# Moving one gate projection among the recurrence levels from behind level 6 to behind level 8 on TensorE

## The reference, cut to what matters

```
for n, o_branch in enumerate((o_mla, o_fnet, o_diff, o_hgrn)):
    gate = sigmoid(gate_logits[..., n * D_MODEL:(n + 1) * D_MODEL])
    merged = merged + gate * (o_branch @ w_branch[l, n])
x = x + merged @ w_out[l]
```

```
cum = cumsum(log_f)
decay = exp(where(lower_tri, cum[t] - cum[s], -inf))
scores = einsum('bhtk,bhtsk,bhsk->bhts', q, decay, k)
intra = einsum('bhts,bhsv->bhtv', scores, v)
```

## Time and profile before

| | |
|---|---|
| median of three runs | 1210.43 us (lowest 1210.18, highest 3123.36) |
| time of the profiled execution | 1210.43 us |
| its span | 1208.6 us |
| TensorE busy | 1190.5 us (98%) |
| VectorE busy | 878.5 us (73%) |
| ScalarE busy | 673.8 us (56%) |
| GpSimd busy | 44.1 us (4%) |
| mean DMA rate | 175 GB/s |

### The profile page before, as it was taken

How to read it: one execution, slowest core, us unless ns; L and a number is a source line. 1 busy time by engine, 2 the same in 40 slices (tenths; PEclk the granted TensorE clock), 3 DMA queues, 4 the chain that set the end, 5 groups by cost and what they waited for, 6 DMA issues and landing times.

```text
span 1208.6 us, 25488 instructions
## 1 busy us (share of the span) xinstructions
PE 1190.5 (98%) x10968; PEld 1154.1 (95%) x10968; DVE 878.5 (73%) x1266; ACT 673.8 (56%) x1077; POOL 44.1 (4%) x90
## 2 busy tenths in 40 slices
PE   8999999999999999999999999999999999999999
PEld 8998999999999999898999999999998999999998
DVE  6998869764457878888876664568788888666644
ACT  5897655443355765592644443557764945444532
POOL 2200200000000000010200000000000100000000
PEclk9999999999999999999999999999999999999999
DMA  9643445555553434442655555544443535555552
GB/s 359 242 148 130 166 144 191 186 205 181 204 175 116 165 133 148 150 166 106 215 200 183 206 197 187 175 174 142 140 161 124 181 131 209 175 201 185 191 192 105
DMA packets 30625, 211.09 MB, mean 175 GB/s; under 512 B 3376, under 2 KB 3760, under 8 KB 5808
## 3 DMA queue, kind: packets, MB, share of 16 engines
q1 hardware_dynamic: 30224, 209.32, 49.9%
q10 hardware_dynamic: 288, 0.14, 0.0%
HBM read 208.39 MB, written 1.05 MB: 173 GB/s over the span
## 4 chain that ended last, share of the span: by engine, by line
PE 78%; ACT 12%; DVE 7%; issue 2%; DMA 1%; SPq 0%; DVEq 0%; ACTq 0%
PE bank L557 76%; ACT w_hi L1244 5%; DVE w_lo L1794 3%; ACT W L1586 2%; ACT W L1244 1%; ACT W L1679 1%; ACT W L1676 1%; ACT W L1678 1%; ACT W L1675 1%; PE bank L938 1%; DMA ring<-weight_pieces 1%; PE bank L677 1%; DVE W L1761 0%; DVE stat L2298 0%; DVE xs L2393 0%
## 5 line engine op out<-in xcount | busy, mean ns | idle before, releaser
L1794 DVE TENSOR_TENSOR w_lo<-ring,w_hi 128x2048 fp32r<-128x2048 f32 (+1 forms) x180 | 409.1, 2273 | 206.3 <-ACT w_hi L1244 204.2
L1244 ACT ACTIVATE w_hi<-ring 128x1024 fp32r<-128x1024 f32 (+1 forms) x368 | 366.4, 1045 | 275.9 <-PE bank L557 245.7
L557 PE MATMUL bank<-x_hi,w_hi 128*128 128x256 f32 x1072 | 159.9, 284 | 2.4 <-issue 1.9
L557 PE MATMUL bank<-x_hi,w_lo 128*128 128x256 f32 x1072 | 152.8, 277 | 4.4 <-DVE w_lo L1794 4.4
L557 PE MATMUL bank<-x_lo,w_hi 128*128 128x256 f32 x1072 | 144.5, 277 | 0.0
L557 PEld LDWEIGHTS bank<-x_hi,w_hi 128*128 128x128 f32 x1072 | 138.4, 189 | 5.8 <-issue 2.2
L557 PEld LDWEIGHTS bank<-x_hi,w_lo 128*128 128x128 f32 x1072 | 136.3, 188 | 5.6 <-DVE w_lo L1794 5.6
L557 PE MATMUL bank<-y_hi,w_hi 128*128 128x256 f32 x992 | 137.9, 277 | 1.3 <-ACT w_hi L1244 1.1
L557 PE MATMUL bank<-y_hi,w_lo 128*128 128x256 f32 x992 | 136.9, 276 | 1.1 <-DVE w_lo L1794 1.1
L557 PEld LDWEIGHTS bank<-x_lo,w_hi 128*128 128x128 f32 x1072 | 132.8, 188 | 0.0
L557 PE MATMUL bank<-y_lo,w_hi 128*128 128x256 f32 x992 | 132.1, 276 | 0.0
(11 more groups left out here) (287 smaller groups left out, 1310.7 us busy)
## 6 DMA issues: line engine op xcount, KB each, us to landing
ring<-weight_pieces SPq DMA_DIRECT2D x191, 1024.0 KB, 4.9
h<-x_features SPq DMA_DIRECT2D x4, 256.0 KB, 5.2
ring<-weight_pieces SPq DMA_DIRECT2D x2, 512.0 KB, 6.4
W<-x SPq DMA_DIRECT2D x2, 512.0 KB, 6.5
W<-rg_weights SPq DMA_DIRECT2D x1, 1024.0 KB, 11.3
xs<-mem_features SPq DMA_DIRECT2D x1, 1024.0 KB, 12.6
oT<-mem SPq DMA_DIRECT2D x1, 1024.0 KB, 14.0
out<-h SPq DMA_DIRECT2D x4, 256.0 KB, 2.0
```

The costliest lines, as they stand in the source:

```text
L557: return nc.tensor.matmul(out, lhsT, rhs, start=first, stop=last)
L1244: return nc.scalar.activation(out, in_, ACT.Copy, scale=scale)
L1794: v.tensor_tensor(whole(w_lo, q), rows, whole(w_hi, q).bitcast(F32), ALU.subtract).then_inc(s_weight_low, 1)
```

## The change

Before, PE ran `gates[5]` directly behind level 5. Now the loop gives PE the gates 0 to 4 as before, nothing behind level 5 or 6, and `gates[5]` behind level 7 (the eighth level, i = 7). The steps of ACT and DVE for this gate keep their places in the list, as does everything else. The number of instructions does not change.

```diff
                 if i + 2 < len(LEVELS):
                     steps += pairs("query", i + 2)
-                if i < 6:
+                if i < 5:
                     steps.append(pe(gates[i]))
+                elif i == 7:
+                    steps.append(pe(gates[5]))
             steps.append(third)
```

## The result

The changed kernel takes 1225.28 us (median of four runs, 1223.63 to 1227.35) against 1210.31 us (median of four): ratio 1.0122, with a 95% interval of 1.0104 to 1.0141, or 12.6 to 17.1 us more. One run of the kernel before, of 3123 us, stands outside all the others (1209.92 to 1210.43 us); the ratio leaves it out, and only the median of four counts it. The profiled execution took 1226.88 us.

What follows compares the result with a forecast made beforehand. PE was taken to bound the kernel. Uncovered gates 10.8, DVE 0.4 and the clock 2.8 summed to 14.0 us on 1210.4: 1224.4 us, 1.2% slower, range 1219.5 to 1228.3.

Steps and rivals of the forecast that it cites:

- ACT sets level 7, and PE can't hurry it: Ahead of level 7: ACT, busy 28.28 of 28.94 us, holds its keys; level 7 starts at 544.54 as before.
- PE idles 1.1 us and then 5.8 us: On PE in layer 0: idle about 1.1 us ahead of level 6, then 5.8 us ahead of level 7.
- The gate, uncovered, costs 4.98 and 5.80 us at full clock, with the issue gap gone: Third merge on PE starts 4.98 us later in layer 0, 5.80 in layer 1; sum 10.8 us.
- the issue gap: PE gap of 0.65 us inside level 8 in layer 0, taken to be gone; add 0.65 if it stays.
- The clock falls in each layer, 1.4 us each: TensorE drops to 1.2 GHz behind PE's gap in each layer: 1.4 us each, 2.8 in all, bounds 0 and 5.6.
- the one fall in the trace: Clock fall from 2.4 to 1.2 GHz after 3.79 us of two-column matmuls from 356.20; priced at 1.42 us.
- slower by over 2%: Rival: clock stays low past gate 5, through third merge, `hval` and gate 6; up to 1270.6 us; chance 0.03.
- The upper bound, 5.6: Clock's share for both layers if the low level meets twice as much dense work: 5.6 us.
- The rival without the fall: Same gaps, but the clock holds at 2.4 GHz: 1221.6 us; chance 0.25, shared with a fall in one layer.
- DVE's merges slip by 0.4 us, 0.2 of it seen ahead of the transposes: DVE behind the gate: some 0.4 us later against PE, slack about 0.2; charged 0.2 us a layer, 0.4 in all.
- not slower: Rival: gate fills the wait ahead of a later level and PE's former idle time goes; 1207.3 us; chance 0.02.

Runs made afterwards that it cites:

- the run with the filled gap: Changed kernel with 40 more gate-wide matmuls on PE ahead of level 7, their result overwritten: 1221.48 us, ratio 1.0088.
- the two kernels: Kernel before with gate 6's high part behind level 7's exponentials, low part behind `near_place`: 1214.85 us; kernel before with tanh of gates 3 and 4 late: 1211.13 us.
- the late scaling: Changed kernel with DVE's scaling of the sixth gate behind the placings and `near_place`: 1224.89 us, ratio 1.0116.
- the kernel with the gate behind level 6: Sixth gate on PE behind level 6 (i = 6) in place of behind level 7 as in the changed kernel: 1209.62 us, ratio 0.9992.
- the changed one with the exponentials first: Changed kernel with gate 6's high part behind level 7's exponentials on ACT, its low part behind level 7's queries on DVE: 1223.66 us, ratio 1.0105.

## Why the prediction was right

It said 1224.4 us, and 1225.3 was measured. Step by step:

- *ACT sets level 7, and PE can't hurry it.* Right: level 7 stands 8.32 us behind level 5 (8.35 before), and it moved by 1.8 us when the order of ACT and DVE was changed, and by 1.0 us when two tanh of ACT alone were. The window of the earlier trace rows runs to 546.96, 2.5 us past the last exponential, into the high part of gate 7; up to 544.44 ACT is busy for 25.78 of 26.42 us, so the reading stands.
- *PE idles 1.1 us and then 5.8 us.* Right: 1.10 and 5.70.
- *The gate, uncovered, costs 4.98 and 5.80 us at full clock, with the issue gap gone.* Right: at full clock, in the run with the filled gap, it is 7.07 and 7.04 us from level 7 to the merge, and 7.08 was worked out.
- *The clock falls in each layer, 1.4 us each.* The mechanism was right, the size was not: 8.92 and 9.71 us less 7.08 are 1.84 and 2.63, 4.5 us in all in place of 2.8. I took the price of the one fall in the trace, and of it only the part on the dense matmuls: 1.42 us, where the rival "slower by over 2%" counts 1.7 us for the same fall. In layer 1 the matmuls of the gate's third group were still slow, which they were not there. The price also differs between executions: over the gaps of 5.7 us in the traces here it is 1.27, 1.32, 1.84, 2.42 and 2.63 us, so 1.4 lies in the range, near its low end. The upper bound, 5.6, held it. The Trainium skill (TensorE: Matmul & The Clock Gate, section "The HAM clock gate") has it that the clock drops when the engine has been idle; the traces now agree for a true gap, with 0.76 and 0.70 behind 5.7 us. The rival without the fall was the run with the filled gap, 1221.5 us against the 1221.6 that it was given.
- *DVE's merges slip by 0.4 us, 0.2 of it seen ahead of the transposes.* Right within a tenth: the last merge instruction of DVE starts 562.00 - 554.23 = 7.77 us behind the third merge on PE, where it was 7.31, and there are 0.29 and 0.24 us more from the merge to the transposes (17.72 in both layers against 17.43 and 17.48).
- *The rival "not slower"*, with the existing idle time won back, failed because level 7 didn't come sooner. Its price was too simple as well: with level 7 early in the kernel before, the time came back as an issue gap in layer 0, and in one of the two kernels as DVE's line behind the levels.

By the trace the sum is 4.98 + 5.80 + 4.5 + 0.5 = 15.8 us, and the median rose by 15.0. The forecast was low by the clock's 1.7 us, and executions that differ by 1 to 2 us hide some of that. That it came within 0.9 us of the median is in part luck: the four runs of the changed kernel lie at 1223.6, 1223.7, 1226.9 and 1227.4.

## What to carry to other kernels

A piece of dense work between short dependent steps is worth its length only in the gap in which the next step's inputs are not ready: find for each neighbour when its last input lands, and what the engine behind that input is busy with. Uncovering one gate of 5.7 us cost more than 5.7 us, because behind a gap of this length the work also ran at the lower clock. And a wait that is removed ahead of a run of very short matmuls may come back inside the run, and bring the clock down in its turn.

## What the runs showed of the hardware

- The clock: idle times of PE of 3.94, 4.09, 5.69 and 5.70 us were each followed by dense matmuls at the lower level (1.2 GHz), one of 2.78 us between dense matmuls and a level was not. But the "issue" gap of 2.01 us was, with only short matmuls around it (PE busy for 2.05 of the 4.06 us from 541.11 to 545.17): granted clock 0.50 from 546.17 to 549.17. The same place with gaps of 1.21 and 0.65 us, or of 0.22 and 1.49, kept 1.00. So the length of a single gap doesn't sort these cases. The loss was 1.3 us at the least (8.35 us from level 7 to the merge in layer 0 with the late scaling, less 7.08) and 2.6 at the most, for the same gap of 5.7 us.
- The stretch of two-column matmuls ahead of layer 0 is the same in all kernels, but the outcome differs. The window of PE over it in the kernel with the gate behind level 6, in the kernel before, and in the changed one with the exponentials first:

```profile
355.00:366.00 11.00, 11.00 (x100) 1.00 0.36 128
```

```profile
355.00:366.00 11.00, 11.00 (x86) 0.84 0.38 140
```

```profile
355.00:366.00 11.00, 11.00 (x71) 0.69 0.32 119
```

  No fall, a short one, a long one: 0.16 and 0.31 of 11 us are 1.8 and 3.4 us of full-speed work. Of the twelve traces three have 1.00, six 0.84 and three 0.69 or 0.75. That is as large as most differences between the kernels here, and it goes with the spread of 1207.9 to 1214.2 us over the 56 runs of the kernel before that stand beside the experiments: the 7 with a mean granted clock of 1.000 took 1208.8 us in the mean, the 29 with 0.999 took 1210.9, and the 17 with 0.997 took 1212.2. A trace of one execution has to be compared stretch by stretch.
- Three levels of 64 short matmul records each in a row (0.70 us each): wherever an "issue" gap stands in them, the last 32 to 48 records start 2.5 to 3.7 us behind the first. In layer 0 the gap is 0.65, 1.49 and 2.01 us where the wait for data before it is 1.21, 0.22 and 0; in layer 1 there is none, 0.50 and 1.05 us where the wait is 1.20, 0.26 and 0. With a dense gate between the three it was never seen. That the supply of instructions to PE is what lags is an inference; no run measured it by itself, nor why the layers differ.
